# Halving the first transfers of an encoder block and multiplying its first strip product by product

## The chip, the cores and the metric

The kernel runs on one NeuronCore of a Trainium2 chip. The metric is the device time of one execution in microseconds. Three executions of the kernel before took 1597.21, 1597.24 and 1597.38 us, median 1597.24 us.

## The reference

One layer of a hybrid encoder block on x of 512 tokens by 2048 features, in float32:

```python
u = rms_norm(h, norm_gain[layer])
proj = jnp.einsum('bsd,de->bse', u, w_in[layer])
(q_sb, k_sb, v_sb, z_sb, q_sa, k_sa, v_sa, z_sa,
 q_ix, k_ix, w_ix, g_sb, g_sa) = jnp.split(proj, splits, axis=-1)
...
mixed = jax.nn.sigmoid(g_sb) * y_sb + jax.nn.sigmoid(g_sa) * y_sa
h = h + jnp.einsum('bsd,de->bse', mixed, w_out[layer])
```

y_sb comes from eight heads of stick-breaking attention, y_sa from eight heads of attention over 128 keys per query that an indexer (q_ix, k_ix, w_ix) chooses; each is gated and projected. A last RMS norm ends it. The change touches only the first columns of proj, those of q_ix, and the loading of x.

## The kernel before, in words

**Precision.** Every large product is done in three matmuls of a reduced type: each operand is split into a high part, rounded to fp32r, and a low part, the rest. A product a*b becomes a_hi*b_hi, a_hi*b_lo and a_lo*b_hi, accumulated in PSUM (mm3, L1177). ScalarE (ACT) writes the high parts, VectorE (DVE) subtracts to get the low parts, TensorE (PE) multiplies.

**Tiling.** The weights are walked in 34 chunks of 512 columns. A chunk has NS = 8 strips of 256 rows, two 128-row tiles j = 0, 1 each. A strip is fetched into `stage` (two buffers), split into `w_hi` and `w_lo` (four buffers) by split_hi (L405) and split_lo (L719), and multiplied in 24 matmuls of 128x512 (4 blocks e, 2 tiles j, 3 products). Strip s of chunk 0 is called strip s here.

**Loading of x.** x is fetched in eight slabs of 256 features (load_x, 512 KB each), slab p into columns 256p on of `xs`. Each slab holds two tiles k = 2p, 2p+1. PE transposes a tile in four 128x128 steps (turn_x, L1221) into a PSUM bank. For k < 4 ACT makes `u_hi` straight from the bank (L440) and DVE makes `u_lo` (L770); then, and for all others, DVE writes the scaled transposed tile to SBUF (turned_raw, L764), which frees the bank. Turns of tiles 4 on reuse banks, so they wait for that.

**The norm** is applied after the first chunk has been started: the first chunk is multiplied with x times gain only. The sums of squares of x come from ACT (sum_of_squares, L456, tile `junk`). The first four of them, over features 0 to 1023 of each of four token blocks, wait for slabs 0 to 3 and stand in ACT's program behind `u_hi` of tile 3 and ahead of the split of strip 2. From the sums DVE derives `rstd`, and PE turns it (L1275) behind strip 4.

**What sets the order.** Each engine's program is written out by hand and runs in order. SyncE (SP) issues, in order: slab 0, strip 0, slab 1, strip 1, slabs 2 to 4, strip 2 (it waits until both halves of strip 0 are split, strip_lo 1), slabs 5 to 7, strip 3 (waits for the split of strip 1, strip_lo 2), the index weights `ixw` (640 KB), and strips 4 on, each waiting for the split two strips before. All of these go through one hardware queue.

**PE's start** (L1242 to L1266): four matmuls on a zeroed tile (keep_busy), the turn of the gain, one keep_busy, turns of tiles 0 and 1, four keep_busy, then first_strip: tile j = 0 in twelve matmuls, turns of tiles 2 and 3, tile j = 1 in twelve matmuls. Then turns of 4 and 5, strip 1, turns of 6 and 7, strip 2, and so on.

**ACT's start** (L468 on): gain, u_hi of tile 0, high part of strip 0 tile 0 (L473), u_hi of tile 1, high part of strip 0 tile 1 (L475), split_hi of strip 1, u_hi of tiles 2 and 3, four sums of squares, split_hi of strip 2. **DVE's start** (L788 on): u_lo of tile 0, low part of strip 0 tile 0 (L791), u_lo of tile 1, low part of tile 1 (L795), turned_raw of tiles 0 and 1, split_lo of strip 1, u_lo of 2 and 3, turned_raw of 2 and 3, split_lo of strip 2, turned_raw of 4 and 5, u_lo of 4 and 5.

Of the kernel before, what the change touches and what calls it, by code (L numbers as in the profile page):

```python
# [30 lines left out]
P = 128  # L31
QT = SEQ // P
KT = D_MODEL // P
CW = 512
# [8 lines left out]
COL_QIX = 8 * HEADS * HD  # L43
# [21 lines left out]
def build(nc, x, norm_gain, w_in, w_branch_sb, w_branch_sa, w_out, final_gain, out):  # L65
    F, R, I = mybir.dt.float32, mybir.dt.float32r, mybir.dt.int32
    ALU, ACT, AX = mybir.AluOpType, mybir.ActivationFunctionType, mybir.AxisListType
# [29 lines left out]
    u_hi = at("u_hi", [KT, SEQ], R, place["u_hi"])  # L97
    u_lo = at("u_lo", [KT, SEQ], R, place["u_lo"])
# [3 lines left out]
    xs = at("xs", [QT, D_MODEL], F, place["area"])  # L102
    stage = at("stage", [2, 2, CW], F, place["stage"])
    w_hi = at("w_hi", [RING, 2, CW], R, place["w_hi"])
# [103 lines left out]
    def sem(name):  # L208
        return nc.alloc_semaphore(name)
# [7 lines left out]
    gain_loaded, ixw_loaded, consts, masks = sem("gain_loaded"), sem("ixw_loaded"), sem("consts"), sem("masks")  # L217
    sumsq, norm_step, rooted = sem("sumsq"), sem("norm_step"), sem("rooted")
    cols_ready, cols_turned, row_ready = sem("cols_ready"), sem("cols_turned"), sem("row_ready")
    first_hi, first_lo = sem("first_hi"), sem("first_lo")  # L220
    raw_ready, raw_scaled, un_hi_ready, un_lo_ready = (
        sem("raw_ready"), sem("raw_scaled"), sem("un_hi_ready"), sem("un_lo_ready"))
# [57 lines left out]
    with block:  # L280

        @block.sync
        def _(sp):
            def load_x(p):
                sp.dma_start(xs[:, :, 2 * P * p:2 * P * p + 2 * P], x_cols[:, :, 2 * P * p:2 * P * p + 2 * P]
                             ).then_inc(x_loaded[p], 16)

            def load_strip(c, s, src):

                if not (isinstance(c, int) and NS * c + s < 2):  # L290
                    sp.wait_ge(strip_lo, c * NS + (s - 1))
                sp.dma_start(stage[:, s % 2, :, :], src).then_inc(strip_loaded[s % 2], 16)

            def load_chunk(c, source, col, moving=False):
                for s in range(NS):
                    load_strip(c, s, source(s)[:, :, ds(col, CW)] if not isinstance(col, int)
                               else source(s)[:, :, col:col + CW])
                    if moving and s == 0:
                        move_squares(c - 1)

            def rows(w):
                return lambda s: w[:, 2 * s:2 * s + 2, :]

            def branch_rows(s):
                return (wsb if s < NS // 2 else wsa)[:, 2 * (s % (NS // 2)):2 * (s % (NS // 2)) + 2, :]

            def first_strip(s):
                load_strip(C_QIX, s, rows(win)(s)[:, :, COL_QIX:COL_QIX + CW])

            load_x(0)  # L310
            first_strip(0)
            load_x(1)
            first_strip(1)
            for p in range(2, 5):
                load_x(p)
            first_strip(2)
            for p in range(5, NS):
                load_x(p)
            first_strip(3)
            sp.dma_start(ixw[:, :, :], win[:, :, COL_KIX:COL_KIX + KW]).then_inc(ixw_loaded, 16)  # L320
            for s in range(4, NS):
                first_strip(s)
            load_chunk(C_QIX + 1, rows(win), COL_QIX + CW)
            def move_squares(c):

                sp.wait_ge(squares_turned, (c + (1 - C_SA)) * QT)
                for a in range(QT):
                    for b in range(QT):
                        sp.dma_start(x_in[SQ * b:SQ * b + SQ, a, :, :], turned[SQ * a:SQ * a + SQ, b, :, :]
                                     ).then_inc(moved, 16)  # L330

            with sp.Fori(C_SB, C_SA + 1) as c:
                load_chunk(c, rows(win), c * CW + (COL_SB - C_SB * CW))
            with sp.Fori(C_SA + 1, C_GATE) as c:
                load_chunk(c, rows(win), c * CW + (COL_SB - C_SB * CW), moving=True)
            with sp.Fori(C_GATE, C_BRANCH) as c:
                load_chunk(c, rows(win), c * CW + (COL_GATE - C_GATE * CW), moving=True)
            load_chunk(C_BRANCH, branch_rows, 0, moving=True)
            with sp.Fori(C_BRANCH + 1, C_OUT) as c:
                load_chunk(c, branch_rows, c * CW - C_BRANCH * CW)  # L340
            with sp.Fori(C_OUT, C_END) as c:
                load_chunk(c, rows(wout), c * CW - C_OUT * CW)

            for i in range(QT):
                for part in (0, 1):
                    cols = slice(Y_CUTS[part], Y_CUTS[part + 1])
                    sp.wait_ge(y_ready[part], i + 1)
                    sp.dma_start(out_rows[i][:, cols], hres[:, i, cols]).then_inc(y_stored, 16)
            sp.wait_ge(y_stored, 16 * 4 * QT)
# [52 lines left out]
        def _(act):  # L402
# [67 lines left out]
            act.wait_ge(gain_ready, 1)  # L470
            turned_high(0)
            act.wait_ge(strip_loaded[0], 16)
            A(w_hi[:, 0, 0, :], stage[:, 0, 0, :], ACT.Copy).then_inc(first_hi, 1)  # L473
            turned_high(1)
            A(w_hi[:, 0, 1, :], stage[:, 0, 1, :], ACT.Copy).then_inc(strip_hi, 1)  # L475
            split_hi(0, 1)
            turned_high(2)
            turned_high(3)
# [237 lines left out]
        def _(dve):  # L716
# [42 lines left out]
            def turned_raw(k):  # L759

                dve.wait_ge(xt_done, k + 1)
                if k == KT // 2:
                    dve.wait_ge(sumsq, QT)
                V.tensor_scalar(raw_u(k), by_tile(turn_bank(k)[:, :]), gain[:, k:k + 1], None,  # L764
                                ALU.mult).then_inc(raw_ready, 1)

            def turned_low(k):
                dve.wait_ge(u_hi_ready, k + 1)
                if k < HEAD_START:
                    V.scalar_tensor_tensor(u_lo[:, k, :], turn_bank(k)[:, :], gain[:, k:k + 1],  # L770
                                           u_hi[:, k, :].bitcast(F), ALU.mult, ALU.subtract).then_inc(u_lo_ready, 1)
                    return
                dve.wait_ge(raw_ready, k + 1)
                V.tensor_tensor(by_tile(u_lo[:, k, :]), raw_u(k), by_tile(u_hi[:, k, :].bitcast(F)),  # L774
                                ALU.subtract).then_inc(u_lo_ready, 1)
# [6 lines left out]
            def normal_low(p):  # L782
                for k in (2 * p, 2 * p + 1):
# [1 line left out]
                    V.tensor_tensor(by_tile(u_lo[:, k, :]), raw_u(k), by_tile(u_hi[:, k, :].bitcast(F)),  # L785
                                    ALU.subtract).then_inc(un_lo_ready, 1)

            dve.wait_ge(gain_ready, 1)  # L788
            turned_low(0)
            dve.wait_ge(first_hi, 1)  # L790
            V.tensor_tensor(w_lo[:, 0, 0, :], stage[:, 0, 0, :], w_hi[:, 0, 0, :].bitcast(F),  # L791
                            ALU.subtract).then_inc(first_lo, 1)
            turned_low(1)
            dve.wait_ge(strip_hi, 1)
            V.tensor_tensor(w_lo[:, 0, 1, :], stage[:, 0, 1, :], w_hi[:, 0, 1, :].bitcast(F),  # L795
                            ALU.subtract).then_inc(strip_lo, 1)
            turned_raw(0)
            turned_raw(1)
            split_lo(0, 1)
# [376 lines left out]
        def _(pe):  # L1176
            def mm3(out_, a_hi, a_lo, b_hi, b_lo, start, stop, free=False):  # L1177
                nc.tensor.matmul(out_, a_hi, b_hi, start=start, stop=False, skip_group_check=free)  # L1178
                nc.tensor.matmul(out_, a_hi, b_lo, start=False, stop=False, skip_group_check=free)  # L1179
                return nc.tensor.matmul(out_, a_lo, b_hi, start=False, stop=stop, skip_group_check=free)  # L1180
# [38 lines left out]
                        steps[s]()  # L1219

            def turn_x(k):  # L1221
                if k % 2 == 0:
                    pe.wait_ge(x_loaded[k // 2], 16)
                if k >= HEAD_START:
                    pe.wait_ge(raw_ready, bank_user(k) + 1)
                for i in range(QT):
                    m = nc.tensor.transpose(turn_bank(k)[:, P * i:P * i + P], xs[:, i, P * k:P * k + P], ident[:, :])
                m.then_inc(xt_done, 1)
# [8 lines left out]
            def keep_busy(n):  # L1237

                for _ in range(n):
                    nc.tensor.matmul(proj[3][:, :], blank[:, 0:P], blank[:, :], start=True, stop=True)  # L1240
# [5 lines left out]
            nc.tensor.transpose(kw_bank[:, 0:KT], gain_rows[0:KT, :], ident[0:KT, 0:KT]).then_inc(gain_turned, 1)  # L1246
            keep_busy(1)
            turn_x(0)
            turn_x(1)
            keep_busy(4)  # L1250

            def first_strip():

                for j in range(2):
                    pe.wait_ge(u_lo_ready, j + 1)
                    if j == 0:
                        pe.wait_ge(first_lo, 1)
                    else:
                        turn_x(2)
                        turn_x(3)  # L1260
                        pe.wait_ge(strip_lo, 1)
                    for e in range(4):
                        cols = slice(P * e, P * e + P)
                        m = mm3(proj[e][:, :], w_hi[:, 0, j, cols], w_lo[:, 0, j, cols],
                                u_hi[:, j, :], u_lo[:, j, :], j == 0, False)
                m.then_inc(strip_used, 1)  # L1266

            def between_strips(s):
# [146 lines left out]
```

## Time and profile before

| | |
|---|---|
| median of three executions | 1597.24 us |
| the profiled execution, its own time | 1597.08 us |
| its span | 1595.5 us |
| PE busy | 1585.0 us, 99% of the span |
| DVE busy | 821.9 us, 52% |
| ACT busy | 572.5 us, 36% |
| mean rate of DMA over the span | 111 GB/s |
| share of PE in the chain that ended last | 97% |

The span is the time between the first and the last recorded instruction; the profiled execution's own time is 1.58 us longer. The matmul records overlap, because matmuls are pipelined: the distance between the starts of neighbours tells the pace, not the duration of one.

### The profile page before, as it was taken

What the parts mean: (1) busy time and instruction counts of PE and PEld (TensorE: products, weight loads), DVE (VectorE), ACT (ScalarE), POOL (GpSimd) and SP (SyncE); (2) the same over time, 40 slices, a digit from 0 to 9 for tenths busy, and PEclk for the clock granted to TensorE, in tenths of its full rate; (3) what the DMA queues carried; (4) which work ended last, traced back from release to release, by engine and by line L of the source; (5) the groups of instructions that cost most, each with busy time, mean ns of one, the idle gap of its engine ahead of it and who ended that gap; (6) DMA issues with size and microseconds to landing.
All of it is one profiled execution on the core that took longest, in us unless ns stands there. A gap on an engine that the chain in (4) does not pass through costs nothing.

```text
span 1595.5 us, 19959 instructions
## 1 busy us (share of the span) xinstructions
PE 1585.0 (99%) x7138; PEld 1317.2 (83%) x7138; DVE 821.9 (52%) x1183; ACT 572.5 (36%) x851; POOL 15.8 (1%) x35
## 2 busy tenths in 40 slices
PE   9999999999999999999999999999999999999997
PEld 7788888888888888888888888888888888888886
DVE  6853678522126655556564546554545545434333
ACT  5542333222224444334453332343332533323232
POOL 0000000000000000000000000000000000000000
PEclk9999999999999999999999999999999999999999
DMA  7223323333333333333334334333433522253223
GB/s 225 82 79 93 93 80 93 106 92 85 100 105 96 111 108 110 111 106 104 106 117 132 109 102 113 98 116 110 115 91 122 181 101 92 96 204 121 98 100 118
DMA packets 97979, 176.39 MB, mean 111 GB/s; under 512 B 11264, under 2 KB 24080, under 8 KB 97296
## 3 DMA queue, kind: packets, MB, share of 16 engines
q1 hardware_dynamic: 93712, 160.60, 33.4%
q0 software_dynamic: 3040, 13.63, 2.3%
q10 hardware_dynamic: 1184, 1.58, 0.3%
q8 instruction: 28, 0.46, 0.1%
q14 instruction: 15, 0.12, 0.0%
HBM read 156.90 MB, written 8.39 MB: 104 GB/s over the span
## 4 chain that ended last, share of the span: by engine, by line
PE 97%; ACT 1%; DVE 1%; DMA 1%; issue 0%; SPq 0%; ACTq 0%; DVEq 0%
PE proj L1178 29%; PE proj L1179 29%; PE proj L1180 29%; PE attn L1179 3%; PE attn L1180 3%; PE attn L1178 3%; DMA xs<-in_x 1%; PE attn L1313 1%; PE attn L1312 1%; ACT junk L463 0%; ACT w_hi L410 0%; DVE w_lo L721 0%; DVE xs L764 0%; DVE area L764 0%; ACT u_hi L443 0%
## 5 line engine op out<-in xcount | busy, mean ns | idle before, releaser
L1178 PE MATMUL proj<-u_hi,w_hi 128*128 128x512 f32 x1536 | 600.5, 391 | 0.5 <-DVE u_lo L774 0.5
L1180 PE MATMUL proj<-u_hi,w_lo 128*128 128x512 f32 x1536 | 598.9, 390 | 0.0
L1179 PE MATMUL proj<-u_lo,w_hi 128*128 128x512 f32 x1536 | 598.8, 390 | 0.0
L721 DVE TENSOR_TENSOR w_lo<-stage,w_hi 128x1024 fp32r<-128x1024 f32 x266 | 323.5, 1222 | 458.7 <-ACT w_hi L410 457.2
L410 ACT ACTIVATE w_hi<-stage 128x1024 fp32r<-128x1024 f32 x266 | 280.1, 1056 | 430.9 <-PE proj L1180 302.2
L1178 PEld LDWEIGHTS proj<-u_hi,w_hi 128*128 128x128 f32 x1536 | 288.8, 188 | 60.2 <-issue 1.3
L1180 PEld LDWEIGHTS proj<-u_hi,w_lo 128*128 128x128 f32 x1536 | 288.5, 188 | 60.2
L1179 PEld LDWEIGHTS proj<-u_lo,w_hi 128*128 128x128 f32 x1536 | 288.8, 188 | 58.7
L1178 PE MATMUL proj<-w_hi,u_hi 128*128 128x512 f32 x256 | 99.9, 390 | 0.0
L1180 PE MATMUL proj<-w_hi,u_lo 128*128 128x512 f32 x256 | 99.8, 390 | 0.0
L1179 PE MATMUL proj<-w_lo,u_hi 128*128 128x512 f32 x256 | 99.8, 390 | 0.0
L426 ACT ACTIVATE area<-proj 128x512 f32 (+1 forms) x80 | 47.8, 598 | 137.5 <-PE proj L1180 137.5
L1179 PE MATMUL proj<-w_lo,area_r 128*128 128x512 f32 x216 | 84.2, 390 | 0.0
L1178 PE MATMUL proj<-w_hi,area_r 128*128 128x512 f32 x216 | 84.1, 390 | 0.0
L1180 PE MATMUL proj<-w_hi,area_r 128*128 128x512 f32 x216 | 84.1, 390 | 0.0
L1005 DVE TENSOR_TENSOR x_lo<-x_in,x_hi 128x1280 fp32r<-128x1280 f32 x16 | 23.9, 1493 | 112.9 <-ACT x_hi L597 112.9
L597 ACT ACTIVATE x_hi<-x_in 128x1280 fp32r<-128x1280 f32 x16 | 20.4, 1275 | 151.9 <-DMA x_in<-turned 151.9
L1179 PEld LDWEIGHTS proj<-w_lo,u_hi 128*128 128x128 f32 x256 | 48.1, 188 | 10.0
L1178 PEld LDWEIGHTS proj<-w_hi,u_hi 128*128 128x128 f32 x256 | 48.1, 188 | 9.9
L1180 PEld LDWEIGHTS proj<-w_hi,u_lo 128*128 128x128 f32 x256 | 48.1, 188 | 9.9
L954 DVE RECIPROCAL og<-og 128x512 f32<-128x512 f32 x16 | 53.6, 3353 | 0.6
L528 ACT ACTIVATE relu<-attn 128x256 f32<-128x256 f32 (+2 forms) x48 | 21.0, 489 | 89.9 <-PE attn L1313 89.9
(175 smaller groups left out, 1413.0 us busy)
## 6 DMA issues: line engine op xcount, KB each, us to landing
stage<-in_w_in SPq DMA_DIRECT2D x208, 512.0 KB, 3.7
stage<-in_w_out SPq DMA_DIRECT2D x32, 512.0 KB, 3.6
x_in<-turned SPq DMA_DIRECT2D x256, 40.0 KB, 1.9
stage<-in_w_branch_sb SPq DMA_DIRECT2D x16, 512.0 KB, 3.6
stage<-in_w_branch_sa SPq DMA_DIRECT2D x16, 512.0 KB, 4.1
xs<-in_x SPq DMA_DIRECT2D x8, 512.0 KB, 8.0
o_scratch<-og POOLq DMA_DIRECT2D x16, 256.0 KB, 2.3
hres<-in_x POOLq DMA_DIRECT2D x1, 4096.0 KB, 13.6
```

The source lines that it names most:

```text
L410: A(w_hi[:, s % RING, :, :], stage[:, s % 2, :, :], ACT.Copy).then_inc(strip_hi, 1)
L426: A(dst(e), proj[e][:, :], ACT.Copy).then_inc(proj_free, 1)
L528: A(relu[:, n % 2, 0:WQ[qi]], attn[h % 4][:, 0:WQ[qi]], ACT.Relu).then_inc(relu_ready, 1)
L597: A(x_hi[:, :, :, :], x_in[:, :, :, :], ACT.Copy).then_inc(pt_hi, 1)
L721: V.tensor_tensor(w_lo[:, s % RING, :, :], stage[:, s % 2, :, :], w_hi[:, s % RING, :, :].bitcast(F), ALU.subtract).then_inc(strip_lo, 1)
L954: V.reciprocal(og[:, :], og[:, :]).then_inc(silu_step, 1)
L1005: V.tensor_tensor(x_lo[:, :, :, :], x_in[:, :, :, :], x_hi[:, :, :, :].bitcast(F), ALU.subtract).then_inc(w_low, 1)
L1178: nc.tensor.matmul(out_, a_hi, b_hi, start=start, stop=False, skip_group_check=free)
L1179: nc.tensor.matmul(out_, a_hi, b_lo, start=False, stop=False, skip_group_check=free)
L1180: return nc.tensor.matmul(out_, a_lo, b_hi, start=False, stop=stop, skip_group_check=free)
L1312: nc.tensor.matmul(o_, q, kix_lo[:, 0:WQ[qi]], start=True, stop=False)
L1313: nc.tensor.matmul(o_, q, kix_hi[:, 0:WQ[qi]], start=False, stop=True).then_inc(dots_done, 1)
```

## The change

The first slab of x and the first strip of W are each fetched in two halves, one per tile k, with semaphores of their own for the first halves. SP's order becomes: x tile 0, W tile 0, x tile 1, W tile 1, slab 1, strip 1, slab 2, strip 2, slabs 3 and 4, strip 3, slabs 5 to 7, `ixw`, strips 4 on. The high part of strip 0 tile 0 moves from ACT to DVE. On PE the turn of tile 1 moves behind the first four products, keep_busy(4) becomes keep_busy(1), and each tile of the first strip is multiplied in three groups of four, w_hi*u_hi, w_hi*u_lo, w_lo*u_hi, each group with its own wait. The number of real matmuls is the same.

```diff
--- before.py
+++ after.py
@@ -217,6 +217,7 @@
+    x_first, first_loaded = sem("x_first"), sem("first_loaded")
@@ -307,16 +308,18 @@
-            load_x(0)
-            first_strip(0)
+            for k, x_sem, w_sem in ((0, x_first, first_loaded), (1, x_loaded[0], strip_loaded[0])):
+                sp.dma_start(xs[:, :, P * k:P * k + P], x_cols[:, :, P * k:P * k + P]).then_inc(x_sem, 16)
+                sp.dma_start(stage[:, 0, k, :], rows(win)(0)[:, k, COL_QIX:COL_QIX + CW]).then_inc(w_sem, 16)
             load_x(1)
             first_strip(1)
-            for p in range(2, 5):
-                load_x(p)
+            load_x(2)
             first_strip(2)
+            load_x(3)
+            load_x(4)
+            first_strip(3)
             for p in range(5, NS):
                 load_x(p)
-            first_strip(3)
@@ -470,9 +473,8 @@
             turned_high(0)
             act.wait_ge(strip_loaded[0], 16)
-            A(w_hi[:, 0, 0, :], stage[:, 0, 0, :], ACT.Copy).then_inc(first_hi, 1)
+            A(w_hi[:, 0, 1, :], stage[:, 0, 1, :], ACT.Copy).then_inc(strip_hi, 1)
             turned_high(1)
-            A(w_hi[:, 0, 1, :], stage[:, 0, 1, :], ACT.Copy).then_inc(strip_hi, 1)
             split_hi(0, 1)
@@ -785,15 +787,17 @@
-            dve.wait_ge(gain_ready, 1)
-            turned_low(0)
+            dve.wait_ge(first_loaded, 16)
+            V.tensor_copy(w_hi[:, 0, 0, :], stage[:, 0, 0, :]).then_inc(first_hi, 1)
             dve.wait_ge(first_hi, 1)
             V.tensor_tensor(w_lo[:, 0, 0, :], stage[:, 0, 0, :], w_hi[:, 0, 0, :].bitcast(F),
                             ALU.subtract).then_inc(first_lo, 1)
-            turned_low(1)
+            dve.wait_ge(gain_ready, 1)
+            turned_low(0)
             dve.wait_ge(strip_hi, 1)
             V.tensor_tensor(w_lo[:, 0, 1, :], stage[:, 0, 1, :], w_hi[:, 0, 1, :].bitcast(F),
                             ALU.subtract).then_inc(strip_lo, 1)
+            turned_low(1)
             turned_raw(0)
@@ -1219,7 +1223,9 @@
             def turn_x(k):
-                if k % 2 == 0:
+                if k == 0:
+                    pe.wait_ge(x_first, 16)
+                elif k == 1 or k % 2 == 0:
                     pe.wait_ge(x_loaded[k // 2], 16)
@@ -1246,23 +1252,29 @@
             keep_busy(1)
             turn_x(0)
-            turn_x(1)
-            keep_busy(4)
+            keep_busy(1)
 
             def first_strip():
 
                 for j in range(2):
-                    pe.wait_ge(u_lo_ready, j + 1)
-                    if j == 0:
-                        pe.wait_ge(first_lo, 1)
-                    else:
+                    def products(w, u, first=False):
+                        for e in range(4):
+                            m = nc.tensor.matmul(proj[e][:, :], w[:, 0, j, P * e:P * e + P], u[:, j, :],
+                                                 start=first, stop=False)
+                        return m
+
+                    if j:
                         turn_x(2)
                         turn_x(3)
-                        pe.wait_ge(strip_lo, 1)
-                    for e in range(4):
-                        cols = slice(P * e, P * e + P)
-                        m = mm3(proj[e][:, :], w_hi[:, 0, j, cols], w_lo[:, 0, j, cols],
-                                u_hi[:, j, :], u_lo[:, j, :], j == 0, False)
+                    pe.wait_ge(u_hi_ready, j + 1)
+                    pe.wait_ge(strip_hi if j else first_hi, 1)
+                    products(w_hi, u_hi, first=j == 0)
+                    if j == 0:
+                        turn_x(1)
+                    pe.wait_ge(u_lo_ready, j + 1)
+                    products(w_hi, u_lo)
+                    pe.wait_ge(strip_lo if j else first_lo, 1)
+                    m = products(w_lo, u_hi)
                 m.then_inc(strip_used, 1)
```

## Rows read from the trace of the kernel before

**Rows 1.** The page: busy time, share of the span and instructions of each engine.

```profile
PE 1585.0 (99%) x7138; PEld 1317.2 (83%) x7138; DVE 821.9 (52%) x1183; ACT 572.5 (36%) x851; POOL 15.8 (1%) x35
```

**Rows 2.** Waits in 0:40 us: engine, line, releaser: us in total, times, longest.

```profile
PE proj L1178 <- DVE u_lo L774: 0.5, 1, 0.5
```

**Rows 3.** Chain that ended last, in order: start us, us, what.

```profile
0.93 0.46 SPq L285
1.45 0.50 SPq L292
1.99 0.47 SPq L285
2.50 0.51 SPq L292
...
3.56 8.94 DMA xs<-in_x
...
26.09 1.14 ACT junk L463 x2
...
41.30 0.89 DVE rstd_cols L819 x4
42.23 0.66 PE attn L1275 x4
```

**Rows 4.** Timeline, ACT and PE around strip 2: start us, us, engine, line, idle before.

```profile
11.96 1.27 ACT L440 ACTIVATE u_hi<-attn,gain 128x512 fp32r<-128x512 f32 x2 [1.38 <-PE attn L1227]
13.11 1.06 ACT L463 ACTIVATE junk<-xs 128x1024 f32<-128x1024 f32 x1
...
22.87 0.47 PE L1178 MATMUL proj<-u_hi,w_hi 128*128 128x512 f32 x1 [0.53 <-DVE u_lo L774]
```

**Rows 5.** DMA issues by window (0.9:1.0, 1.9:2.1, 2.4:2.6): size, us to landing.

```profile
xs<-in_x SPq DMA_DIRECT2D x1, 512.0 KB, 3.9
...
stage<-in_w_in SPq DMA_DIRECT2D x1, 512.0 KB, 5.3
xs<-in_x SPq DMA_DIRECT2D x1, 512.0 KB, 6.2
...
stage<-in_w_in SPq DMA_DIRECT2D x1, 512.0 KB, 7.0
```

**Rows 6.** Tile xs, SP alone, 4.0:4.3: slab 4's issue (ns) and landing (us).

```profile
L285 SPq DMA_DIRECT2D xs<-in_x x1: 1811/1811/1811, 4.2 to 4.2; - x1
DMA to landing us min/median/max: 9.8/9.8/9.8
```

**Rows 7.** Timeline of SP: the issue of strip 2.

```profile
9.49 0.37 SPq L292 DMA_DIRECT2D stage<-in_w_in  x1
```

**Rows 8.** Timeline of PE, its start and the first turns after it.

```profile
4.02 0.80 PE L1240 MATMUL proj<-blank 128*128 128x512 f32 x1
4.83 1.97 PE L1227 MATMUL attn<-ident,xs 128*128 128x128 f32 x8
6.45 2.05 PE L1240 MATMUL proj<-blank 128*128 128x512 f32 x4
8.35 0.59 PE L1178 MATMUL proj<-u_hi,w_hi 128*128 128x512 f32 x1
8.78 0.39 PE L1179 MATMUL proj<-u_lo,w_hi 128*128 128x512 f32 x1
9.01 0.40 PE L1180 MATMUL proj<-u_hi,w_lo 128*128 128x512 f32 x1
```

**Rows 9.** Timeline of ACT and DVE, first high and low parts, low parts of tiles 2 and 3.

```profile
6.04 0.69 ACT L440 ACTIVATE u_hi<-attn,gain 128x512 fp32r<-128x512 f32 x1 [1.73 <-PE attn L1227]
7.52 0.68 DVE L791 TENSOR_TENSOR w_lo<-stage,w_hi 128x512 fp32r<-128x512 f32 x1
...
12.68 1.41 DVE L770 SCALAR_TENSOR_TENSOR u_lo<-attn,gain,u_hi 128x512 fp32r<-128x512 f32 x2 [0.77 <-ACT u_hi L440]
```

**Rows 10.** Busy time by stretch: us, PE, PEld, DVE, ACT, POOL, granted clock, DMA.

```profile
0.00:5.00 5.00, 3.23 (x7) 1.80 (x8) 0.83 (x10) 1.47 (x2) 1.22 (x9) 1.00 0.53 181
```

## The prediction

> **What bounds the kernel now.** I read the page first: PE is busy for 1585.0 us, 99% of the span [rows 1]. A change at the start can only win what PE loses there, some 10 us in all, and 8.35 us of that lie ahead of the first real matmul [rows 8]. Next the waits: after that matmul PE waits once, 0.5 us, ahead of strip 2 [rows 2, 4]. Then the chain that ended last. It does not run through PE at the start. Followed back from the turn of rstd at 42.23 us it goes through DVE and ACT to the four sums of squares and to a DMA of x, issued at 3.56 us and landed at 3.56 + 8.94 = 12.50 us [rows 3]. That DMA is slab 3: slab 4 is the next one, issued at 4.2 us [rows 6]. So the end of the kernel hangs on two things: PE's own work from 8.35 us on, and the ACT and DVE sequence that begins when slab 3 is there. In the 0.5 us wait at 22.87 us it is the second that counts, and again at 42.23 us, where the last piece before PE's turn is DVE's rstd_cols [rows 3, 4]. Behind that PE does not wait.
>
> How slab 3 enters: the sums wait for slabs 0 to 3 and stand behind u_hi of tile 3, so they begin at the later of two times. Before, these are 12.5 us (landing) and 13.11 us (u_hi done) [rows 3, 4]: slab 3 has 0.6 us to spare.
>
> **The start of PE, part by part.** Slab 0 lands at 0.93 + 3.9 = 4.83 us [rows 3, 5], and the turn starts at once [rows 8]. Its first half lands earlier, but PE has one blank matmul from 4.02 us, and blanks go 0.43 us apart there (8.35 to 8.78 us is one such distance [rows 8]), so turn 0 starts at 4.45 us at the earliest: 0.38 us won. If the half landed no earlier than the whole, nothing is won; I take 4.45, because half of the bytes are asked for. u_hi of tile 0 starts 6.04 - 4.83 = 1.21 us behind the turn and takes 0.69 [rows 8, 9]: 5.66 to 6.35 us. The first half of W has to be there and copied by DVE. It is the first 512 KB in the queue, where slab 0 was, so about 4.85 us; the copy has no row of its own, the nearest is the subtraction of the same shape, 0.68 us [rows 9], and the bounds are 0.3 and 1.2 us. Copy and subtraction end at 6.2 us, ahead of u_hi, which covers them; at the upper bound the first products start 0.1 us later if anything.
>
> The first four products run from 6.47 us, 0.43 us apart, to 8.18 us. Before, the first real one began at 8.35 us. The three blanks taken out are worth nothing in themselves: they stood in idle time. Turn 1 (its half lands near 6 us) takes four steps of 0.2 us, 1.62 us for eight by 4.83 to 6.45 us [rows 8], a little less if the pace doubles on the way. Then come eight products 0.23 us apart (8.78 to 9.01 us [rows 8]) to 10.7 us. Turns 2 and 3, which before began at 11.32 us after twelve products, begin at 10.7 us. So PE is 0.6 us ahead, and stays so through the same 12 + 24 matmuls and turns.
>
> DVE gets 0.7 us more at the start (the copy), and u_lo of tile 1 comes after u_hi of tile 1 at 9.8 us, for its turn now follows four products. DVE's following work slips by about 1.2 us (low parts of tiles 2 and 3 done at some 15 us in place of 12.68 + 1.41 = 14.1 [rows 9]), and PE wants them for strip 1 at about 15.1 us (10.7 us, turns of 0.8, twelve products of 2.8, turns of 0.8). That fits narrowly; if it doesn't, PE loses what is missing out of its own lead only.
>
> **The queue of transfers.** Here the sum turns. The transfers land one after another: slab 0 at 4.83 us, strip 0 at 1.45 + 5.3 = 6.75, slab 1 at 1.99 + 6.2 = 8.2, strip 1 at 2.50 + 7.0 = 9.5 us [rows 3, 5], slab 3 at 12.5 and slab 4 at 4.2 + 9.8 = 14.0 us [rows 3, 6]. Some 1.3 to 1.5 us for each 512 KB, without a gap: here the DMA engines are the limit. Slab 3 was sixth in this line. In the new order strip 2 stands ahead of it, so it is seventh, where slab 4 was: 14.0 us. SP's own wait ahead of strip 2 (strip_lo 1) ends earlier than the issue at 9.49 us [rows 7] did: high part of W tile 1 on ACT after 6.8 us, low part on DVE to 8.3 us. Behind that wait stand slabs 3 and 4. It opens at 8.4 us while strip 1 (9.5 us) and slab 2 behind it still fill the engines, so no hole arises; an opening as late as 9.5 us would cost nothing either. The next wait, strip_lo 2 at about 13.2 us, holds strip 3 and slabs 5 to 7. The second sums, which want these slabs, come at 26.09 us [rows 3]; four turns of 1.45 us behind slab 4 end at about 21 us.
>
> The two extra issues cost SP 0.5 us each [rows 3], hidden behind the backlog (slab 4's issue took 1811 ns because the queue was full [rows 6]). Halving slab 0 makes its pieces 512 bytes in place of 1 KB. No row has this. Slabs in 1 KB pieces take 1.45 us (6.75 to 8.2), strips in 2 KB pieces 1.3 us (8.2 to 9.5): the step from 2 KB to 1 KB costs 0.15 us. I take 0.2 us for the next step, once. The lower bound is 0 (even -0.1, if the first transfers start up more smoothly), the upper 0.7 us, if the half slab takes as long as the whole one, half of a 1.45 us turn.
>
> The Trainium skill, "DMA: Bandwidth & Descriptors", section Specifications, puts the smallest piece at full rate at 512 bytes. No row here shows it; by it the 0.2 us would be 0 and the result 0.2 us lower.
>
> **The sum.** Slab 3 lands at 14.0 + 0.2 = 14.2 us. u_hi of tile 3 is done at about 12.5 us, so the sums now wait for the slab, 14.2 in place of 13.11 us: +1.1 us. Everything that follows in this chain keeps its durations: four sums, the split of strip 2, its low part, the raw tiles 4 and 5, their high and low parts. PE starts strip 2 at 22.87 + 1.1 = 24.0 us, though it is ready for it at 21.7 us. Its lead of 0.6 us goes into a longer wait, 2.2 us in place of 0.5. From there on PE is full again [rows 1, 2], and the turn of rstd at 42.23 us slips by the same 1.1 us, as its chain does. Against the profiled execution's own 1597.08 us (span 1595.5 and 1.58 around it) that makes 1598.2 us; the median of the runs is 0.16 us above the profiled one, so 1597.24 + 1.1 = 1598.3 us. The case's own range is 1597.9 to 1598.9 us (0 to 0.7 for the pieces).
>
> **Rivals.**
>
> *Slab 3 comes in time.* If a free share of DMA bandwidth took in strip 2 without moving slab 3, or the sums were not what the chain hangs on, PE's lead would count: the sums would begin at 12.5 us in place of 13.11, strip 2 and all after it 0.6 us earlier, 1596.6 us. For it: 0.5 to 0.6 us of lead on both PE and ACT. Against it: evenly spaced landings that leave no free share. It decides only if slab 3 lands before 13.1 us.
>
> *Half and half.* Strip 2 moves slab 3 by less than a turn, to 13.1 to 13.5 us, because the halved start fills the queue sooner. Then 1597.2 to 1597.6 us, as before.
>
> *PE's clock stays low.* The row grants 1.00, 2.4 GHz, from the start on [rows 10], yet blanks and first products go 0.43 us apart until 8.78 us and 0.23 us after [rows 8]; the spacing tells of the level of 1.2 GHz until about 8.6 us, behind the turns and two of the four blanks. The change takes three blanks out, and PE idles from some 6.1 to 6.5 us. If the clock then rises only during tile j = 1, products stay 0.43 us apart: eight of them end at 12.4 us, turns 2 and 3 at 13.2, u_hi of tile 3 at 14.7 us, which is now later than slab 3. The chain starts at 14.7 in place of 13.11: +1.6 us, 1598.8 us. It decides from u_hi of tile 3 past 14.2 us. Should the low level last through strip 1, 24 more products at 0.43 us bring strip 2 to 30.3 us: +7.5 us, 1604.7 us.
>
> The Trainium skill, "TensorE: Matmul & The Clock Gate", Part 4: PE-mode transpose, says that transposes do not count as work towards the higher clock. By it, the blanks taken out are the very work that raised it, and this rival would gain. That the clock rose only behind four blanks, not behind the eight turns [rows 8], agrees.
>
> **How the numbers follow.** Forecast 0.62; slab 3 in time 0.12; half and half 0.12; low clock to j = 1 0.11; low clock through strip 1 0.03. The likeliest time is 1598.3 us. The range, 1597.0 to 1599.2 us, takes in the forecast, the in-between case and most of the first low-clock case, and leaves out the gain and the long low clock. A difference under 0.2%, 3.2 us, can't be told from none in a measurement of this kernel. Only the long low clock is slower by more: 0.03. Nothing here gains 3.2 us: 0.01 for what I don't see. The rest, 0.96, is within.
>
> **What the profile after would show.** Turn 0 at 4.4 to 4.5 us; four products before 8.3 us; the distance between products falling from 0.43 to 0.23 us near 8.6 us; slab 3 landing at about 14.2 us and the first sum of squares starting right there, with an ACT idle ahead of it that names the DMA; PE's wait ahead of strip 2 at about 2.2 us, and strip 2 starting at 24.0 us. The prediction is wrong if slab 3 lands before 13.5 us, if strip 2 starts earlier than 22.87 us, or if a new wait arises ahead of strip 1.

## The result and the profile after

The changed kernel takes 1601.15 us, median of 13 executions (1598.93 to 1603.32), beside 1597.38 us for the kernel before (13, 1596.98 to 1598.12): ratio 1.0022, 95% interval 1.0015 to 1.003. It is slower by 3.8 us where 1.1 were forecast, and its executions lie 4.4 us apart where those of before lie 1.1 apart. The profiled execution is the fastest of them, 1598.93 us (span 1597.3). Three executions far outside all others, 5778 us of e13, 1987 us of e16 and 3255 us of the kernel before beside them, are left out of every figure below.

The chain of the changed kernel that ended last, in order (start us, us, what), which answers to [rows 3]:

```profile
2.46 5.24 DMA stage<-in_w_in
7.72 0.64 ACT w_hi L476
8.39 0.70 DVE w_lo L798
9.11 0.37 SPq L293
9.52 5.35 DMA xs<-in_x
14.97 1.16 ACT junk L466 x2
...
19.67 0.96 ACT w_hi L413
20.65 1.23 DVE w_lo L723
...
43.16 0.89 DVE rstd_cols L823 x4
44.10 0.66 PE attn L1287 x4
```

Slab 3 is still in the chain, but now it has a history: it was issued only at 9.52 us (before, at 3.56), because SP stood at the wait for both halves of strip 0 ahead of strip 2's issue at 9.11 us. The second half of W landed at 2.46 + 5.24 = 7.7 us, a microsecond after the whole strip had before. Slab 3 lands at 14.87 us, the sums start at 14.97 in place of 13.11 us, and the turn of rstd comes at 44.10 in place of 42.23 us.

PE's timeline (start us, us, engine, line, idle before), which answers to [rows 4, 8]:

```profile
4.47 1.05 PE L1233 MATMUL attn<-ident,xs 128*128 128x128 f32 x4
5.18 0.78 PE L1246 MATMUL proj<-blank 128*128 128x512 f32 x1
6.37 2.08 PE L1262 MATMUL proj<-u_hi,w_hi 128*128 128x512 f32 x4 [0.42 <-ACT u_hi L443]
8.24 1.06 PE L1233 MATMUL attn<-ident,xs 128*128 128x128 f32 x4
8.95 2.00 PE L1262 MATMUL proj<-u_lo,w_hi 128*128 128x512 f32 x4
10.79 1.08 PE L1262 MATMUL proj<-u_hi,w_lo 128*128 128x512 f32 x4
11.70 1.03 PE L1233 MATMUL attn<-ident,xs 128*128 128x128 f32 x8
...
22.59 0.66 PE L1233 MATMUL attn<-ident,xs 128*128 128x128 f32 x4 [0.33 <-DVE area L766]
24.73 0.47 PE L1182 MATMUL proj<-u_hi,w_hi 128*128 128x512 f32 x1 [1.48 <-DVE u_lo L776]
```

The start does what the change says: turn 0 at 4.47 us, four products from 6.37 us. Strip 2 begins at 24.73 us, 1.86 us later than the 22.87 of [rows 4], and 1597.08 + 1.86 = 1598.94 us is this execution's time. So in its fastest execution the whole loss stands ahead of strip 2, where PE waits twice, for tile 7's bank (0.33 us) and for the low parts of strip 2 (1.48 us), 1.81 us in place of 0.53.

PE is not ahead when it comes there. Turns 2 and 3 begin at 11.70 us; in the kernel before they begin earlier, although its first product is two microseconds later:

```profile
11.32 1.03 PE L1227 MATMUL attn<-ident,xs 128*128 128x128 f32 x8
```

The reason is PE's clock: in this execution four products still take 1.8 us (8.95 to 10.79 us), the level of 1.2 GHz, while before they went 0.23 us apart from 8.78 us on.

### The profile page after: what moved, and what is told of

Same layout as the page of the kernel before. It is cut to its first block, busy times and chain, and to the rows that moved or that the text cites. A ratio compares the mean times of both kernels' runs of the same rounds, so it can differ in the third digit from the quotient of the medians.

```text
span 1597.3 us, 19955 instructions
## 1 busy us (share of the span) xinstructions
PE 1585.3 (99%) x7135; PEld 1316.1 (82%) x7135; DVE 822.3 (51%) x1184; ACT 572.1 (36%) x850; POOL 15.8 (1%) x35
## 4 chain that ended last, share of the span: by engine, by line
PE 97%; ACT 1%; DVE 1%; DMA 1%; issue 0%; SPq 0%; ACTq 0%; DVEq 0%
PE proj L1182 29%; PE proj L1183 29%; PE proj L1184 29%; PE attn L1183 3%; PE attn L1184 3%; PE attn L1182 3%; PE attn L1325 1%; PE attn L1324 1%; ACT junk L466 0%; DMA xs<-in_x 0%; DMA stage<-in_w_in 0%; ACT w_hi L413 0%; DVE w_lo L723 0%; DVE area L766 0%; ACT u_hi L446 0%
```

## Experiments

Each was timed beside the kernel before, whose medians were 1597.25 us (e1 to e8), 1597.16 us (e9 to e12) and 1597.47 us (e13 to e16). A blank is one matmul of keep_busy on the zeroed tile. The theories are named in the expectations: C puts the loss down to PE's clock and the blanks taken out, Q to slab 3's landing alone, P to the size of the pieces, N to the number of transfers, F to the clock falling in the wait ahead of strip 2.

**e1, three blanks out, and e2, three blanks back.** Edits, to the kernel before and to the changed one:

```diff
             turn_x(1)
-            keep_busy(4)
+            keep_busy(1)
```
```diff
             turn_x(0)
-            keep_busy(1)
+            keep_busy(4)
```

> The kernel before with one edit: keep_busy(4) ahead of the first strip becomes keep_busy(1), as in the change; transfers and products stay as before. Theory C (the three blank matmuls taken out let PE's clock rise late and at a varying time): median 1598.5 to 1602 us, executions spread over more than 2 us, clock share of the slow ones 0.998 or less. Theory Q (the changed kernel is slower by the landing of slab 3 alone): 1597.4 us as before, spread under 1.2 us.

> The changed kernel with keep_busy(4) put back between turn 0 and the first products. Theory C: the spread closes to about 1 us and what is left is the queue's part, slab 3 landing at 14.9 us in place of 12.5 and the sums starting 1.8 us late: 1599.2 us. Theory Q: the blanks don't matter, so as the changed kernel, 1601 us with a spread of 4 us.

e1: 1598.9 us (1597.05 to 1599.38, 11 executions), interval of the ratio 1.0001 to 1.0019. Theory C holds there. e2: 1601.58 us (1600.84 to 1602.83, 8 executions). Theory C fails: blanks back cure nothing, so what they cost alone is not what the changed kernel loses. Theory Q has the time, but not the spread (2.0 us for 4). Two traces tell why. In e2's, PE waits for tile 7's bank and again ahead of strip 2, and the granted clock of 22 to 30 us is 0.79 (columns: stretch; us; busy us of PE, PEld, DVE, ACT, POOL; clock; DMA):

```profile
22.00:30.00 8.00, 5.01 (x17) 3.92 (x18) 7.36 (x10) 4.50 (x7) 0.00 (x0) 0.79 0.78 202
```

**e10, three blanks out, second look.**

> The kernel before with three blanks out once more, for the trace of an execution near its median (1598.9 us; the one profiled was its fastest, 1597.05, clock up at 7.66 us). Theory C: time 1598.4 to 1599.4 us, and the granted clock is low for about 3 us more than in the kernel before, either up only at 11 to 12 us or down again in between. Rival: the clock is as before and a wait or a transfer explains the 1.7 us.

1599.01 us. PE's timeline:

```profile
8.53 0.77 PE L1178 MATMUL proj<-u_hi,w_hi 128*128 128x512 f32 x1 [1.18 <-DVE w_lo L791]
9.09 0.63 PE L1179 MATMUL proj<-u_lo,w_hi 128*128 128x512 f32 x1
9.52 0.63 PE L1180 MATMUL proj<-u_hi,w_lo 128*128 128x512 f32 x1
...
12.08 0.59 PE L1180 MATMUL proj<-u_hi,w_lo 128*128 128x512 f32 x1
12.51 0.40 PE L1178 MATMUL proj<-u_hi,w_hi 128*128 128x512 f32 x1
```

After an idle of 1.18 us the products go 0.43 us apart, the level of 1.2 GHz, until 12.5 us; in e1's own trace, of its fastest execution, they went 0.23 us apart from 8.77 us. So the blanks are worth 1.7 us in a kernel whose PE then has nothing to do. In the changed kernel PE waits ahead of strip 2 in any case, so a late clock costs nothing there until that wait is gone (e7).

**e3, order of before back, and e4, new order alone.** The edit of e4 to the kernel before; e3 is its reverse in the changed one:

```diff
-            for p in range(2, 5):
-                load_x(p)
+            load_x(2)
             first_strip(2)
+            load_x(3)
+            load_x(4)
+            first_strip(3)
             for p in range(5, NS):
                 load_x(p)
-            first_strip(3)
```

> The changed kernel with the later transfers in the order of before (slabs 2 to 4, strip 2, slabs 5 to 7, strip 3), the first two still halved. Theory Q: slab 3 lands at about 13.5 us, sums start 0.4 us late: 1597.8 us with a spread under 1.2 us. Theory C: the fastest executions come down by 1 us or more, to some 1597.8, but the spread of 3 us or more stays, median 1599 to 1600.5 us.

> The kernel before with only the order of the later transfers changed (slab 2, strip 2, slabs 3 and 4, strip 3, slabs 5 to 7). Slab 3 is seventh and lands at 14.0 us, 0.9 us after the sums began before. Theory Q: 1598.3 us, spread under 1.2 us; and theory C the same, since the blanks are in. If the order is harmless: 1597.4 us.

e3: 1598.03 us (1597.7 to 1598.25, 11), slab 3 landing at 13.89 us. e4: 1599.66 us (1599.21 to 1603.73, 11), ratio 1.001 to 1.0028. The order alone brings 2.4 us and a spread of 4.5 us; with the order of before the changed kernel loses 0.8 us (an interval that takes in 1: 0.9995 to 1.0013) and its executions lie 0.6 us apart. Theory Q named the right place, but neither e4's time nor its spread, and its slab 3 lands at 15.56 us, not at 14.0. Its chain:

```profile
9.97 5.59 DMA xs<-in_x
15.67 1.16 ACT junk L464 x2
```

The sums start 2.56 us later than before, and 1597.08 + 2.56 = 1599.64 us (measured in this execution: 1599.66). The same distance ties the two in every trace that has the old sums: strip 2 begins 9.75 or 9.76 us behind the start of the first sum (before 13.11 and 22.87 us, changed 14.97 and 24.73, e4 15.67 and 25.42). The missing 1.5 us are a hole in the transfers. What the DMA engines moved from 10 to 11 us, in the kernel before, in e4 and in the changed kernel:

```profile
DMA packets 361, 0.36 MB, mean 359 GB/s; under 512 B 10, under 2 KB 361, under 8 KB 361
```
```profile
DMA packets 44, 0.07 MB, mean 66 GB/s; under 512 B 4, under 2 KB 20, under 8 KB 44
```
```profile
DMA packets 151, 0.19 MB, mean 191 GB/s; under 512 B 11, under 2 KB 105, under 8 KB 151
```

Before, slabs 3 and 4 lay in the queue when SP's wait opened at 9.5 us. In the new order they stand behind the wait, and only slab 2 is left to cover it. The engines are nearly empty for some 0.6 us of e4's hole (37 GB/s from 10.00 to 10.25 us, 25 from 10.25 to 10.50). Behind that they move 203 and 287 GB/s from 11 to 13 us at a busy share of 0.82 and 0.85, in place of 347 and 351; why they are slow to come back was not found.

**e8, slab 0 by tile, e9, slab 0 by token blocks, e6, slab 0 whole.** e6 is the changed kernel with slab 0 whole and the later transfers in the order of before. e8 and e9 fetch slab 0 of the kernel before in two transfers, both awaited, in pieces of 512 bytes and of 1 KB:

```diff
-            load_x(0)
+            for k in range(2):
+                sp.dma_start(xs[:, :, P * k:P * k + P], x_cols[:, :, P * k:P * k + P]).then_inc(x_loaded[0], 16)
```
```diff
+            for k in range(2):
+                sp.dma_start(xs[:, 2 * k:2 * k + 2, 0:2 * P], x_cols[:, 2 * k:2 * k + 2, 0:2 * P]).then_inc(x_loaded[0], 16)
```

> The kernel before with slab 0 fetched in two transfers by tile (pieces of 512 bytes), both awaited as one; nothing else changed. Theory P: slab 3 lands up to 1 us later, at 13.5 us, sums 0.4 us late, turn 0 starts later too (5.5 us), 1597.7 to 1598.3 us. If pieces of 512 bytes run at full rate: 1597.4 us.

> The kernel before with slab 0 fetched in two transfers by token blocks (256 KB each, pieces still 1 KB), both awaited as one. The same split by tile (pieces of 512 bytes) gave a median of 1600.05 us and strip 0 landing at 8.6 in place of 6.75 us. Theory P (the pieces): strip 0 lands at 6.8 to 7.3 us, 1597.3 us. Theory N (one more transfer ahead in the queue): strip 0 at 8 us or later, 1599 us or more.

e8: 1600.05 us (1597.94 to 1600.33, 11), ratio 1.0003 to 1.0022. e9: 1598.69 us (1598.37 to 1600.45, 11), ratio 1.0004 to 1.0022. Theory P fell: e9 has whole pieces of 1 KB and loses too. The two issues and strip 0 behind them, in e9 (size, us to landing; issued at 0.93, 1.45 and 1.95 us), and strip 0 in e8 (issued at 1.99 us):

```profile
xs<-in_x SPq DMA_DIRECT2D x1, 256.0 KB, 3.0
...
xs<-in_x SPq DMA_DIRECT2D x1, 256.0 KB, 3.2
...
stage<-in_w_in SPq DMA_DIRECT2D x1, 512.0 KB, 6.3
```
```profile
stage<-in_w_in SPq DMA_DIRECT2D x1, 512.0 KB, 6.6
```

The halves are in by 4.7 us (e9) and 4.8 us (e8), as slab 0 was whole. But strip 0 lands at 8.2 us with pieces of 1 KB and at 8.6 us with 512 bytes, in place of 6.75. One more small transfer at the head costs what lies behind it 1.4 us, of which 0.5 us is the later issue (1.95 for 1.45 us). Whether the further 0.4 us of e8 are the piece is not shown, with one trace each. Theory N has e9's landing (8 us or later); its 1599 us or more is missed by 0.3 us.

Here it is PE that comes late, not slab 3. It waits 1.94 us (e8) and 1.56 us (e9) for the low part of strip 0. The executions of both fall into two groups, near 1598.5 and near 1600.2 us (five and six in e8, six and five in e9), and the traces, of a slow one of e8 and a fast one of e9, show what parts them. The first two lines and the stretch are e8's, the last line is e9's:

```profile
10.08 0.47 PE L1179 MATMUL proj<-u_hi,w_hi 128*128 128x512 f32 x1 [1.94 <-DVE w_lo L792]
14.50 1.04 PE L1228 MATMUL attn<-ident,xs 128*128 128x128 f32 x8
11.00:14.00 3.00, 3.00 (x9) 2.32 (x8) 2.73 (x4) 1.06 (x1) 0.00 (x0) 0.50 1.10 354
12.57 1.03 PE L1228 MATMUL attn<-ident,xs 128*128 128x128 f32 x8
```

In e8 the granted clock, once up, falls again behind the wait. Its first product is 0.35 us later than e9's (9.73 us), the turns behind the first twelve are 1.93 us later: 1.6 us of the 1.88 us between the two executions are the clock. The medians fall into different groups, so their distance of 1.4 us says nothing of the piece.

> The changed kernel with slab 0 in one transfer and the later transfers in the order of before; W's first strip still in halves, PE's program as changed. Against the run with only the order put back (1598.03 us, slab 3 at 13.9 us) this differs by the 512 byte pieces alone. Theory P (small pieces cost the queue 1.4 us): slab 3 lands at 12.5 us, sums at 12.5 to 12.9 us, median 1596.7 to 1597.0 us. Theory N (the number of transfers, not the piece, costs it): slab 3 at 13.4 us or later, 1597.5 to 1598 us.

e6: 1597.64 us (1596.94 to 1598.31, 11), slab 3 at 4.00 + 9.32 = 13.32 us. Theory N has the time and misses the landing by 0.1 us: with only W halved slab 3 is 0.8 us late, with slab 0 halved too (e3) 1.4 us.

**e11, the changed kernel, second look.**

> The changed kernel unchanged, for a second trace, if it can be of an execution at or above its median (1601.15 us; the one profiled before was its fastest, 1598.93, with slab 3 at 14.9 us and the clock up once, at 10.75 us). Theory: slab 3 lands at 15 to 16.5 us, and where the time is above 1600 us the clock falls once behind the wait ahead of strip 2. Rival: slab 3 lands at 14.9 us again and the rest is PE's clock at the start.

1601.56 us, near the median. Chain, PE's timeline, and busy time by stretch:

```profile
9.44 6.58 DMA xs<-in_x
```
```profile
19.78 0.60 PE L1233 MATMUL attn<-ident,xs 128*128 128x128 f32 x4
23.73 1.11 PE L1233 MATMUL attn<-ident,xs 128*128 128x128 f32 x4 [3.36 <-DVE area L766]
25.87 0.76 PE L1182 MATMUL proj<-u_hi,w_hi 128*128 128x512 f32 x1 [1.02 <-DVE u_lo L776]
```
```profile
23.00:30.00 7.00, 5.25 (x14) 4.04 (x15) 6.58 (x10) 4.28 (x6) 0.00 (x0) 0.52 0.60 167
```

Slab 3 lands at 16.02 us and strip 2 begins 3.0 us late. PE waits 3.36 and 1.02 us. The clock falls toward the end of the first wait, and the granted clock of 23 to 30 us is 0.52, the level of 1.2 GHz. PE works at half pace for part of strip 2, which takes 8.13 us (to strip 3 at 34.00 us) in place of 6.33 (22.87 to 29.20 us): another 1.8 us. Together 4.8 us; measured 4.5, since a wait of 0.26 us that PE had at the turn of rstd (41.97 to 42.23 us) is eaten on the way. The theory is confirmed. Here the clock at the start was up early, turns 2 and 3 began at 9.69 us, and PE came to strip 2's turns 1.5 us ahead of the kernel before (19.78 for 21.30 us); it only waited longer.

**e5, e13 and e17, the waits filled.** e5 puts six blanks behind the turns of tiles 6 and 7; e13 and e17 (the same kernel again) put twelve between them:

```diff
                     turn_x(2 * s + 4)
+                    if s == 1:
+                        pe.wait_ge(raw_ready, 4)
+                        for _ in range(12):
+                            nc.tensor.matmul(kw_bank[:, :], blank[:, 0:P], blank[:, :], start=True, stop=True)
                     turn_x(2 * s + 5)
```

> The changed kernel with six blank matmuls added behind the turns of tiles 6 and 7, into a free PSUM bank, so that PE works through most of its wait ahead of strip 2 (in the changed kernel some 1.5 to 2.2 us there). Theory F (in many executions the clock falls to the lower level because of this wait, and that is the 1600 to 1603 us part): executions gather at 1598.9 to 1599.4 us, spread under 1.5 us. Theory C (the clock rises late at the start, because of the three blanks taken out): no change, 1601 us and a spread of 4 us.

> The changed kernel with twelve blank matmuls (2.7 us) between the turns of tiles 6 and 7, where its second trace waits 3.4 us with the clock falling at 22.9 us. Theory F: slab 3 still lands at 15 to 16 us, but the clock stays up, and executions gather at 1599 to 1600.2 us, no time above 1600.7 us. Rival (slab 3's landing alone makes the 1601 to 1603 us): median 1601.3 us and up to 1603 as in the changed kernel.

> The changed kernel with twelve blanks between the turns of tiles 6 and 7, once more for its trace. Theory F: slab 3 lands at 15 to 16 us, the clock goes up once (5 to 12 us) and does not fall before the end of the kernel; PE's wait for tile 7 is under 1 us; 1599.3 to 1600.6 us. Rival: the clock falls between 20 and 30 us all the same.

e5: 1600.34 us (1599.35 to 1602.72, 11), which neither theory forecast; the six stood behind PE's long wait. Its trace has the clock up throughout, slab 3 landing at 9.53 + 6.64 = 16.2 us, strip 2 at 26.03 us, 3.16 us late, and a time of 1600.34 us: 1597.08 + 3.26. So slab 3's landing alone makes over 3 us in some executions. e13: 1599.74 us (1599.34 to 1601.03, 11), without a trace of its own. The median is 1.4 us under the changed kernel's and the spread 1.7 in place of 4.4 us: theory F in the main, with two executions above its bound. The mean granted clock of each execution agrees: none of e13's is below 0.998, while the changed kernel's three slowest (1602.52 us and more) have 0.996 or 0.997 and its four fastest 0.999. e17, meant to show it, doesn't: 1601.69 us, with the clock down again, as the row and PE's wait show.

```profile
25.00:30.00 5.00, 3.81 (x10) 3.02 (x11) 4.71 (x7) 3.02 (x5) 0.00 (x0) 0.66 0.51 158
```
```profile
24.06 0.66 PE L1233 MATMUL attn<-ident,xs 128*128 128x128 f32 x4 [0.51 <-DVE area L766]
26.19 0.50 PE L1182 MATMUL proj<-u_hi,w_hi 128*128 128x512 f32 x1 [1.48 <-DVE u_lo L776]
```

The blanks took up the first wait, not the second (1.48 us), and the clock falls just behind it. The forecast for this run failed. By e13's times filling makes the low clock rarer; by e17 it doesn't rule it out.

**e7 and e12, the sums moved off strip 2's path,** in the changed kernel and in the kernel before:

```diff
+SUMS = {0: ((0,), (1,)), 1: ((2,), (3,)), 2: ((4,), (5, 6)), 3: ((7,), ())}
...
-            for i in range(QT):
-                sum_of_squares(i, 0)
...
+                    ahead, behind = SUMS.get(s, ((), ()))
+                    for i in ahead:
+                        sum_of_squares(i % QT, i // QT)
                     if s + 2 < NS:
                         turned_pair(s + 2)
-                    if s in (1, 2):
-                        for i in (2 * s - 2, 2 * s - 1):
-                            sum_of_squares(i, 1)
-                    elif s == 3:
+                    for i in behind:
+                        sum_of_squares(i % QT, i // QT)
+                    if s == 3:
```

> The changed kernel, transfers as changed, with the eight sums of squares moved on ACT: none ahead of the split of strip 2, one ahead of and one behind the high parts of each following pair. Strip 2 then no longer hangs on slab 3. Theory Q (the loss is slab 3's landing handed on by the sums): PE starts strip 2 at about 22 us without a wait, median 1596.3 to 1597 us, spread under 1.2 us. Rival (the loss is in PE's own start, its clock or its waits): 1599 us or more remains.

> The kernel before with only the eight sums of squares moved on ACT (none ahead of strip 2's split). PE's waits of 0.5 us ahead of strip 2 and 0.1 to 0.3 us at the turn of rstd go: 1596.5 to 1596.8 us. If the change's own start is worth something beyond that, the changed kernel with the sums moved (1596.28 us) must be below this one.

e7: 1596.28 us (1595.15 to 1596.51, 11). The changed kernel, with its order and its hole, loses nothing: 4.9 us under its own median and 1.0 under the kernel before (ratio 0.9983 to 1.0001, which takes in 1). All its waits of PE in the first 60 us, and the first product of strip 2:

```profile
PE proj L1247 <- DVE blank L756: 1.7, 1, 1.7
PE proj L1263 <- ACT u_hi L444: 0.4, 1, 0.4
```
```profile
22.32 0.47 PE L1183 MATMUL proj<-u_hi,w_hi 128*128 128x512 f32 x1
```

e12: 1596.36 us (1595.93 to 1597.04, 11), 0.1 us under its forecast. The changed start is worth 0.1 us, not told from nothing.

**e14 to e16, variants of the start, sums moved.** e14: slab 0 and strip 0 whole, transfers in the old order, keep_busy(4), products as changed. e15: e7 with keep_busy(4). e16: only W in halves, old order.

> Sums moved as in the runs with 1596.3 us; slab 0 and strip 0 fetched whole, all transfers in the order of before; PE's products one by one as changed, keep_busy(4) kept, the first high part of W on DVE. Strip 0 lands at 6.75 us, first products at 7.3 to 7.4 us in place of 8.35: 1595.5 to 1596.0 us. If the first products are worth nothing: 1596.4 us, as the kernel before with the sums moved.

> The changed kernel with the sums moved and keep_busy(4) put back. Theory C in small: the blanks lift the clock at 5 to 8.6 us in place of 10.4 us, worth up to 1.2 us, against 1.3 us in which they might hold up the first products only while the clock is low: 1595.3 to 1596.2 us. If the first products lift the clock as well as blanks do: 1596.3 us or above.

> The changed kernel with the sums moved, slab 0 whole, strip 0 in halves, later transfers in the order of before, keep_busy(1). First products at 6.8 us. PE-bound from there: 1595.8 to 1596.6 us, between the changed kernel and the kernel before, both with the sums moved (1596.28 and 1596.36 us).

e14: 1596.35 us (1595.58 to 1596.94, 11), as its rival said: the earlier first products are worth nothing. e15: 1596.08 us (1595.42 to 1596.58, 11), ratio to the kernel before 0.9981 to 0.9999. e16: 1596.40 us (1595.86 to 1597.04, 11). The five kernels with moved sums lie within 0.3 us, whatever their start. e15 is the lowest median and below both kernels, 1.4 us under the one before by the medians of its own batch (1.2 us by those of the first eight runs).

Two things in the traces use up the earlier start. In e7 and e14 it is the clock. It comes up later (four products take 1.7 us from 8.94 us in e7), and strip 2 begins at 22.32 and 22.37 us, behind the 22.09 us of e12. In e15 the blanks stand ahead of the first products, the clock is up when these begin, and strip 2 begins a microsecond ahead of e12's. There PE waits at the turn of rstd. Strip 2 of e12, strip 2 of e15, and e15's turn of rstd:

```profile
22.09 0.48 PE L1179 MATMUL proj<-u_hi,w_hi 128*128 128x512 f32 x1
21.03 0.48 PE L1183 MATMUL proj<-u_hi,w_hi 128*128 128x512 f32 x1
41.17 0.65 PE L1288 MATMUL attn<-ident,rstd_cols 128*128 128x128 f32 x4 [0.86 <-DVE rstd_cols L824]
```

In e12 that turn is at 41.21 us, without a wait. So the next bound is the chain to rstd.

## Why the prediction was wrong

The sign, the place and the carrier were right: slab 3's landing is handed on by the four sums of squares, and nothing that PE gains at its start passes the wait ahead of strip 2 (e4, e7, e11). The size was off: 3.8 us at the median against 1.1, outside the range.

*"So no hole arises; an opening as late as 9.5 us would cost nothing either."* This is the step that failed. The wait opened at 9.1 us (8.4 was forecast), inside the bound of 9.5, and the hole was there: 191 GB/s at 10 to 11 us in place of 359. I took it that strip 1 and slab 2 would keep the engines full, and left out the time from an issue to its first bytes: the first issue, at 0.93 us, moves nothing before 2.0 us. With the order changed in the kernel before, the hole costs 1.5 us (e4: 15.56 us in place of 14.0), part of it the empty engines, part their slow return.

*"I take 0.2 us for the next step"*, for the smaller pieces. The term was sought in the wrong thing. Not the size of the piece but one more small transfer at the head of the queue costs most (e9: 1.4 us for strip 0). There the 0.5 us of an extra issue are not *"hidden behind the backlog"*, for none has formed yet, and SP's wait opens later as well (e9: 10.87 for 9.49 us). In the order of before, both halvings move slab 3 by 1.4 us (e3), W's alone by 0.8 (e6), where 0.2 were forecast. The terms do not add up: e4's 3.1 us and e3's 1.4 stand against 2.4 to 3.8 us in the traces of the changed order, and how the two act together was not taken apart.

*"So PE is 0.6 us ahead, and stays so"* failed too, without a cost here. It takes the pace of 0.23 us from 9.0 us on for granted. In the fastest execution the slow pace lasts to 10.75 us and PE is 0.4 us behind (turns 2 and 3 at 11.70 for 11.32 us), in e11 the first four products are already fast (6.36 to 7.40 us) and PE is 1.6 us ahead. Both end in the wait.

*"PE's clock stays low"* was a rival, but at the wrong place. The three blanks do matter by themselves (e1, 1.7 us), as its working says. In the changed kernel a late clock at the start is covered by the wait. The clock that costs time is the one that falls at the longer wait ahead of strip 2, which I had forecast at 2.2 us and given no price. In e2, e11 and e17 it falls there, in the first trace of the changed kernel and in e5 not. It is the second cost of the same delay: 1.5 to 1.8 us in those executions, by the length of strip 2. How the median's 3.8 us divide is known from single traces only: e5, with the clock up, is 3.3 us over the kernel before, e11, with it down, 4.5. No trace was taken of an execution above 1601.7 us.

The sign seen in *"the clock rose only behind four blanks, not behind the eight turns"* was weak. At the first product, 8.35 us, all four blanks had begun, and in e1's trace the fast pace is there at 8.77 us behind the eight turns and one blank. No run isolates the turns.

Right in the rest: turn 0 at 4.47 us (4.45), products from 6.37 us (6.47), slabs 5 to 7 in time, PE full behind strip 2. The new wait ahead of strip 1, named as a sign of being wrong, is absent in both traces of the changed kernel and there, 0.2 to 0.4 us long, in e2, e5 and e17; it is lost in the longer wait behind it. Of u_hi as the cover for W's split, right: DVE had both parts by 5.6 us. The forecast landing of slab 3 at 14.2 us is refuted by every trace of this order: 14.9 to 16.3 us. Why it varies by 1.4 us from one execution to the next stays open. In four traces with late landings (15.8 to 16.3 us) the clock rose early, at 5.0 to 6.0 us (e2, e5, e11, e17), and with the earliest (14.9 us) late, at 10.75 us; but e7 has both late (10.4 and 15.9 us), and no experiment varied that by itself.

## What to carry to other kernels

When a transfer is moved behind a wait of its queue's issuer, ask what is still in flight when the wait opens, and set against it the time from an issue to its first bytes. Here one slab of 512 KB was in flight and did not cover it, so all that stood behind the wait was late by the hole as well as by its place. An engine with slack on one side of a wait gains nothing from being earlier; find what ends the wait first (here four sums that nobody needed yet) and move that. And a wait of PE can cost more than its length, since the clock may fall at it: here it did in part of the executions (e2, e8, e11, e17).

## What the runs showed of the hardware

The granted clock fell in e11 during a PE wait of 3.36 us (0.52 from 23 to 30 us), in e8 behind a single wait of 1.94 us (0.50 from 11 to 14 us), in e17 behind waits of 0.51 and 1.48 us (0.66 from 25 to 30 us). In e5 a wait of 3.29 us, followed by six blanks, left it up. Whether it falls is not fixed for a kernel: of the two traces of the changed kernel one has the drop and one hasn't. Nor is the time of its rise at the start: 5.8 and 10.75 us in these two. Two transfers of 256 KB in place of one of 512 KB land together as early as the one (4.7 us), yet the transfer behind them lands 1.4 us later (e9); from 4 to 8 us the engines move less (e9: 278 GB/s from 4 to 5 us, e8: 138, in place of 370). What holds them up there was not found.
